# Two feed-forward steps and the end of a recurrent block in another order, and the first weights cast by VectorE

## What is computed

```
def _sq_relu_mlp(x, w1, w2):
    return jnp.square(jax.nn.relu(x @ w1)) @ w2

y = (b_gate * conv3(c_gate * h)) @ w_out                  # layer 1, [b_gate, c_gate, h] = x @ w_in
x = _layer_norm(ALPHA * x + y, ln_mix_g[i], ln_mix_b[i])  # layers 1 and 2
x = _layer_norm(ALPHA * x + _sq_relu_mlp(x, ff_w1[i], ff_w2[i]), ln_ff_g[i], ln_ff_b[i])
x = x + gate[:, None, :] * y                              # layers 3 and 4
k, v = jnp.split(h @ w_kv, 2, axis=-1)                    # h: x normed, scaled and shifted
```

## Time and profile before

| | us |
|---|---|
| median of the timed runs (3) | 780.31 |
| lowest and highest | 780.28, 780.37 |
| the profiled execution, in all | 780.2 |
| its span, from the first to the last instruction | 778.4 |
| TensorE busy in it | 768.9 |
| VectorE busy | 586.1 |
| ScalarE busy | 405.1 |
| GpSimd busy | 34.6 |

### The profile page before, as it was taken

One profiled execution on the slowest core, in us unless ns is written; L12 is line 12 of the kernel. 1 busy time (PEld: TensorE's weight loads), 2 busy tenths in 40 slices (PEclk: granted clock), 3 DMA queues, 4 the chain that ended last, 5 costly groups with the idle time before them and its releaser, 6 DMA issues.

```text
span 778.4 us, 12084 instructions
## 1 busy us (share of the span) xinstructions
PE 768.9 (99%) x4982; PEld 697.1 (90%) x4982; DVE 586.1 (75%) x786; ACT 405.1 (52%) x512; POOL 34.6 (4%) x66
## 2 busy tenths in 40 slices
PE   9999999999999999999999999999999999999996
PEld 9999888988998889888889988998799988999995
DVE  5886898868688697687989776676687877756754
ACT  5455235545445424875355444445649869664632
POOL 0000000000000001000000000000500051000001
PEclk9999999999999999999999999999999999999999
DMA  9877438897867731446488977876235254754102
GB/s 351 319 274 278 184 125 324 348 320 289 313 231 288 290 122 62 163 139 267 165 326 344 347 273 275 308 263 245 103 109 216 109 216 163 270 216 164 55 3 80
DMA packets 26983, 173.94 MB, mean 223 GB/s; under 512 B 3248, under 2 KB 3632, under 8 KB 7856
## 3 DMA queue, kind: packets, MB, share of 16 engines
q1 hardware_dynamic: 26640, 173.14, 60.0%
q10 hardware_dynamic: 288, 0.02, 0.0%
HBM read 172.10 MB, written 1.05 MB: 222 GB/s over the span
## 4 chain that ended last, share of the span: by engine, by line
PE 93%; DVE 3%; ACT 2%; POOL 1%; issue 0%; POOLq 0%; ACTq 0%
PE bank L578 12%; PE bank L580 12%; PE bank L579 12%; PE Y L714 10%; PE Y L716 10%; PE Y L713 10%; PE bank L1067 2%; PE bank L1068 2%; PE bank L1069 2%; PE bank L996 2%; DVE w_low L1610 1%; PE bank L816 1%; PE Y L738 1%; PE bank L610 1%; PE bank L619 1%; PE bank L611 1%
## 5 line engine op out<-in xcount | busy, mean ns | idle before, releaser
L1610 DVE TENSOR_TENSOR w_low<-raw,w_high 128x2048 fp32r<-128x2048 f32 (+3 forms) x125 | 278.5, 2238 | 65.1 <-ACT w_high L1203 62.8
L1203 ACT CAST w_high<-raw 128x2048 fp32r<-128x2048 f32 (+3 forms) x125 | 232.5, 1869 | 92.9 <-DMA raw<-weights 80.0
L578 PE MATMUL bank<-xT_h,w_high 128*128 128x256 f32 x728 | 206.5, 284 | 0.1
L579 PE MATMUL bank<-xT_l,w_high 128*128 128x256 f32 x728 | 205.8, 283 | 0.0
L580 PE MATMUL bank<-xT_h,w_low 128*128 128x256 f32 x728 | 205.8, 283 | 0.0
L578 PEld LDWEIGHTS bank<-xT_h,w_high 128*128 128x128 f32 x728 | 139.4, 192 | 1.6 <-DVE w_low L1610 0.3
L579 PEld LDWEIGHTS bank<-xT_l,w_high 128*128 128x128 f32 x728 | 139.4, 191 | 1.1
L580 PEld LDWEIGHTS bank<-xT_h,w_low 128*128 128x128 f32 x728 | 139.5, 192 | 0.0
L714 PE MATMUL Y<-w_low,hT_h 128*128 128x512 f32 x324 | 128.3, 396 | 0.0
L713 PE MATMUL Y<-w_high,hT_h 128*128 128x512 f32 x324 | 128.0, 395 | 0.0
L716 PE MATMUL Y<-w_high,hT_l 128*128 128x512 f32 x324 | 101.9, 395 | 0.0
(11 more groups left out here) (291 smaller groups left out, 1144.5 us busy)
## 6 DMA issues: line engine op xcount, KB each, us to landing
raw<-weights SPq DMA_DIRECT2D x149, 1024.0 KB, 5.0
rows<-rows_in SPq DMA_DIRECT2D x9, 512.0 KB, 7.7
raw<-weights SPq DMA_DIRECT2D x4, 576.0 KB, 3.5
z<-gates_in SPq DMA_DIRECT2D x4, 512.0 KB, 3.8
raw<-weights SPq DMA_DIRECT2D x2, 896.0 KB, 4.4
raw<-weights SPq DMA_DIRECT2D x3, 512.0 KB, 7.0
x<-x_in SPq DMA_DIRECT2D x2, 512.0 KB, 4.4
kT<-rows_in SPq DMA_DIRECT2D x2, 512.0 KB, 8.3
```

The source lines that it names most:

```text
L578: mm(dst, high, xh[:, kt, :], start=kt == 0, stop=False)
L579: mm(dst, high, xl[:, kt, :], start=False, stop=False)
L1203: nc.scalar.copy(w_high[:, n % RING, start:COLS[n]], raw[:, s % RAW, start:COLS[n]]).then_inc(w_high_ready, 1)
L1610: tt(w_low[:, n % RING, start:COLS[n]], slot[:, start:COLS[n]], f32(w_high[:, n % RING, start:COLS[n]]), ALU.subtract).then_inc(raw_done, 1)
```

## The change

It has three parts.

1. In both feed-forwards, TensorE's order: the first half of group 2's block 0 is done ahead of the transposes of block 1, the second half behind them, and in the same way the first half of group 2's block 1 ahead of `turn_pair` of the first pair.
2. At the end of rg, the splits of the value pieces: VectorE makes the low part of the second piece ahead of the gated residual, the third where the second stood, and the fourth where the third stood. ScalarE casts the third ahead of the squares and the fourth where the third stood.
3. At the beginning, the high part of the first 512 columns is made by VectorE in place of ScalarE (semaphore `first_high`), and the low part of the next 512 columns by GpSimd in place of VectorE (semaphore `second_low`). SyncE waits for `second_low` before it loads into that raw buffer again.

The diff, without the lines that declare the two semaphores:

```diff
             for s, (kind, n) in enumerate(STREAM):
                 if s >= RAW:
                     sp.wait_ge(raw_done, s - RAW + 1)
+                if s == RAW:
+                    sp.wait_ge(second_low, 1)
...
-                    pe.wait_ge(half_high, k0 // 4 + 1)
+                    pe.wait_ge(half_high if k0 else first_high, 1)
...
-                    pe.wait_ge(half_low, k0 // 4 + 1)
+                    pe.wait_ge(second_low if k0 else half_low, 1)
...
                 if n == 1:
-                    pe.wait_ge(half_low, 3)
+                    pe.wait_ge(half_low, 2)
...
                 pair_block(first[0], phase, 0, fresh)
+                up_block(first[2], PI[phase, "up", 2], 0, fresh, range(0, KT // 2))
                 transposes(fresh, x, "x_ready", [1])
-                up_block(first[2], PI[phase, "up", 2], 0, fresh)
+                up_block(first[2], PI[phase, "up", 2], 0, fresh, range(KT // 2, KT))
                 pair_block(first[1], phase, 1, fresh)
+                up_block(first[2], PI[phase, "up", 2], 1, fresh, range(0, KT // 2))
                 turn_pair(phase, 0)
                 in_order(phase, 2)
-                up_block(first[2], PI[phase, "up", 2], 1, fresh).then_inc(product, 1)
+                up_block(first[2], PI[phase, "up", 2], 1, fresh, range(KT // 2, KT)).then_inc(product, 1)
                 turn_pair(phase, 1)
...
+            pool.wait_ge(half_high, 1)
+            nc.gpsimd.tensor_tensor(w_low[:, 0, 512:PIECE // 2], raw[:, 0, 512:PIECE // 2],
+                                    w_high[:, 0, 512:PIECE // 2].bitcast(F32), ALU.subtract).then_inc(second_low, 1)
             pool.wait_ge(ident_in_done, 16)
...
-            part_high(0, 0, 0, 512)
             await_transposed(act, "init", 1, 1)
...
-            split_ahead(("rg", "down", MXG - 1), 2)
+            split_ahead(("rg", "down", MXG - 1), 3)
             rms_squares("rs2", "rg", 0)
...
-            split_ahead(("rg", "down", MXG - 1), 3)
+            split_ahead(("rg", "down", MXG - 1), 4)
             gate_kept(0)
             rms_squares("rs2", "rg", 1)
-            split_ahead(("rg", "down", MXG - 1), 4)
             rms_scale("rs2", 1)
...
-                dve.wait_ge(half_high, part + 1)
+                if part == 0:
+                    dve.wait_ge(first_high, 1)
+                else:
+                    dve.wait_ge(half_high, part)
...
             low_transposed("init", 0)
+            dve.wait_ge(part_in[0], 16)
+            nc.vector.tensor_copy(w_high[:, 0, 0:512], raw[:, 0, 0:512]).then_inc(first_high, 1)
             for q in range(2):
...
-                part_low(q, 0, q * 512, (q + 1) * 512)
+                if q == 0:
+                    part_low(0, 0, 0, 512)
...
-            split_ahead(("rg", "down", 3), 1)
+            split_ahead(("rg", "down", 3), 2)
             gated_residual("rg", 0, 0)
             await_rstd("rs2", 0)
-            split_ahead(("rg", "down", 3), 2)
+            split_ahead(("rg", "down", 3), 3)
```

1 line of the change is left out of this document (added).

## The result

The changed kernel takes 782.01 us in the median, beside 780.32 for the kernel before on the same chip: a ratio of 1.0019, with an interval of 1.0012 to 1.0025, or +1.5 us (+0.9 to +2.0); the two medians by themselves are 1.7 us apart. One of the 18 timed runs took 1526 us, the other 17 took 781.0 to 782.6; it doesn't move the median. The forecast was 781.5, in a range of 780.5 to 782.7. By the bound of 0.2% this is right at the edge between no change and slower.

A forecast was written before the change was run, and what follows sets the result against it. TensorE, busy 768.9 of 778.4 us, was taken as the bound. Terms 0.66 + 0.34 − 0.13 + 0.34 = +1.21 us; 780.2 + 1.2 + 0.1 = 781.5 us, range 780.5 to 782.7.

The forecast's parts named there:

- ff1, +0.66: Second feed-forward: removing the wait for x gives 0.84 us, later VectorE work up to turned_low(1) takes back 1.50.
- ff0, +0.34: First feed-forward: no wait to remove; later turn_pair(0) and ScalarE's cast delay turned_low, so down(0, 1) starts +0.34 us.
- The end of rg, −0.33 + 0.20: Value pieces: wait for v2's w_low goes, −0.33 us; GpSimd's columns wait out VectorE's w_low, root +0.20 us.
- The beginning, +0.34: GpSimd's subtraction holds VectorE's big low part until 11.07, so the second tile starts at 12.34, not 12.00: +0.34 us.
- (b): Beginning: GpSimd and VectorE don't hold each other; second tile at 11.91, −0.09 us, in all 781.1; chance 0.16.
- (a): Beginning: GpSimd gets in ahead of VectorE's first low part; second tile 12.98, +0.98 us, in all 782.2; chance 0.26.
- Rival (d): Beginning: GpSimd shut out, losing to VectorE piece by piece; second tile at 15.4, +3.4 us, in all 784.6; chance 0.08.
- Rival (c): Feed-forwards: VectorE takes the later transposes without being late; sum −1.26 us, in all 779.0; chance 0.08.
- the wait before turn_pair(1): Sign in ff1: TensorE waits about 0.65 us for VectorE before turn_pair(1), in place of the wait for x.
- those before down(0, 1): Sign in both feed-forwards: TensorE waits for VectorE before down(0, 1).
- ff1's down(0, 1) 0.3 us farther from ff0's: Sign across the feed-forwards: the distance between the two down(0, 1) starts grows by 0.3 us.
- the second tile at 12.3: Sign at the beginning: the second tile at 12.3 us, with a GpSimd subtraction of 1.8 us including its wait.

The follow-up runs named there:

- ff_only: Part 1 alone (TensorE's order in both feed-forwards) on the kernel before: 781.61 us, ratio 1.0016.
- half_a: Kernel before with only part 1's half block ahead of the transposes of x: one run, ff0 +0.40, ff1 +0.74 us.
- half_b: Kernel before with only part 1's half block ahead of turn_pair of the first pair: one run, ff0 +0.52, ff1 +0.46 us.
- rg_columns_early: Part 2 on the kernel before, plus GpSimd spreading the second gate's columns into buf_a after the recurrent layer's first quarter: 779.82 us, ratio 0.9991.
- ff_late_mod: Part 1 on the kernel before, plus VectorE's modulation piece ahead of group 2's squares moved behind turned_low(1): 780.68 us, ratio 1.0001.
- start_only: Part 3 alone (the beginning) on the kernel before: 780.56 us, ratio 1.0001.
- rg_and_between: Kernel before with parts 1 and 2, one VectorE weight piece behind turned_low(0), the rest behind turned_low(1), GpSimd's columns early: 779.78 us, ratio 0.9994.
- hold: Kernel before plus four extra GpSimd 128x512 two-input subtractions beside VectorE's work at the beginning: one run, second tile at 14.08 us.
- all_repaired: All three parts on the kernel before, with ff_squares_first's VectorE order and rg_columns_early's edit: 780.91 us, ratio 1.0008.
- ff_squares_first: Part 1 on the kernel before, plus VectorE's weight and modulation pieces between the squares put off behind turned_low(1): 781.02 us, ratio 1.0005.
- rg_only: Part 2 alone (the value pieces at the end of rg) on the kernel before: 780.29 us, ratio 0.9998.

## Why the prediction was right, and where not

**ff1, +0.66: right, measured +0.75.** Each step is in the rows: the wait for x gone, xT_l at 379.34, 2.69 us behind the last of the pair's products (376.65), by the forecast 378.39 − 375.69 = 2.70. Down to turned_low(1) nothing gave. From the pair's end to down(0, 1) it is 393.92 − 376.65 = 17.27 us, and was 392.29 − 375.69 = 16.60: +0.67. Of the rest, 0.1 is the restart: down(0, 1)'s first products are 0.57 us apart behind the wait (393.40 and 393.97 in ff_only) and 0.48 without one. half_a shows that the late xT_l alone does it.

**ff0, +0.34: right, measured +0.50.** From the pair's end (107.55, the 106.64 of its low products plus 0.91) to down(0, 1) it is 123.67 − 107.55 = 16.12 us, beside 122.82 − 107.06 = 15.76: +0.36, and 0.1 for the same restart. half_b shows that the path named, by `turn_pair` and the cast, costs this by itself. What the forecast didn't see is that half_a alone costs +0.40 too, though its own terms say so: xT_l comes 1.44 us later and finds 0.21 us of idle time, which leaves 1.23, beside 1.24 by way of the cast. The delayed xT_l brings turned_low(0) to the same time (118.94 and 118.96), so undoing either half alone would not have saved ff0.

**The end of rg, −0.33 + 0.20: the mechanism right, the second term mis-sized.** The wait for v2 went, for −0.41 (the 0.33, and a restart that went with it). GpSimd did wait out the added w_low. But the forecast let it in between VectorE's two pieces, and had the root 0.2 us late. One column lasted 4.52 us, through both of them; the root came 643.22 − 632.15 = 11.07 us behind the first column, and was 640.89 − 630.42 = 10.47 behind it: 0.6 us late, not 0.2. In the stage table the transposes of z are 0.44 late. The sum is +0.03, where the forecast had −0.13. rg_columns_early takes the collision away and leaves −0.43, which settles it.

**The beginning, +0.34: the number came near (+0.48) by luck, its reason did not take place.** The step that failed is the time at which the operations meet. The forecast took ScalarE's times from the earlier trace rows; in the changed kernel everything behind the second x block is some 0.6 us later, because its load is. GpSimd starts at 9.97, beside an xT_l with an input in PSUM. By the time it is through (11.30), VectorE's big low part has just started, at 11.20, held by ScalarE's cast and that by its load. None of VectorE's operations there is longer than in the earlier trace rows by more than 0.01 us, so of the rivals (b) fits the edit best. (a) did not occur: VectorE's first low part starts at 9.46, 0.5 us ahead of GpSimd.

What the 0.48 us measure is two late loads. TensorE's first tile, late by x, runs up to the second one without idle time. And the load of the rest of piece 0 would have put the second tile there by itself: ScalarE's cast waits for it until 10.12, and the same delay stands in ff_late_mod and in rg_columns_early, which have the old beginning. Of ff_late_mod:

```profile
10.08 1.05 ACT L1205 CAST w_high<-raw 128x1024 fp32r<-128x1024 f32 x1 [0.31 <-DMA raw<-weights]
...
12.44 0.39 PE L578 MATMUL bank<-xT_h,w_high 128*128 128x256 f32 x1 [0.43 <-DVE w_low L1612]
```

From the start of this cast to the second tile it is 2.36 or 2.37 us in ten of the fourteen profiles, the changed kernel, start_only and eight with the old beginning. It is 2.42 in the kernel before, 2.54 in rg_and_between, 4.37 in `hold`, and 2.53 in all_repaired, the one place where part 3's own hold shows: 0.16 us. Measured from the first tile instead, the second comes 2.97 us later in the changed kernel and 3.16 in the one before. That says little, since with the old beginning it is 3.09 to 3.57, by when the loads came.

That the two engines hold each other was right, as `hold` shows, and the Trainium skill, page "SBUF — State Buffer", section "SBUF: two separate sides", says it: of a GpSimd operation and a VectorE operation with two inputs in SBUF, whichever starts first has the shared ports for its whole instruction. The runs agree: 1.0 us for each VectorE operation beside one of GpSimd's, and none for the one with a PSUM input.

What stays open is why the loads come when they do. For the weights the spread is there with the old beginning too. TensorE transposes the second x block at 7.54, 7.60 and 7.16 in the three profiles with part 3, and at 6.19 to 7.02 in the six others whose rows show it apart. Part 3 changes nothing that comes before these loads in any queue. With three profiles the late x can be chance; or it can be something that the trace doesn't show. The timed runs of start_only put it and everything else of part 3 within 0.7 us of nothing.

**Rival (d)**, GpSimd shut out for long, is refuted for two-input operations: in `hold` they go by turns. **Rival (c)** fell by ff0 and ff1, as above.

**What would show it.** Of the signs, the wait before turn_pair(1) came as 0.51 us of idle time, or 0.66 from start to start, and those before down(0, 1) came as well. One sign was miscounted: the forecast has ff1's down(0, 1) 0.3 us farther from ff0's, but ff0's shift moves both, so by its own terms it is 0.66. Measured it is (393.92 − 123.67) − (392.29 − 122.82) = 0.78. The sign that the second tile at 12.3 speaks for the hold was no test, since the loads alone put it at 12.44 and 12.47 in kernels with the old beginning.

**The range and the chances.** The parts sum to +1.76 us in the profile and the timed runs show +1.5. Against the profile the forecast's +1.21 was low by 0.25 in the feed-forwards (0.2 of it two restarts), by 0.16 at the end of rg, and by 0.14 at the beginning. Without the beginning, the parts sum to 1.76 − 0.48 = 1.28 us. The forecast had 0.66 + 0.34 − 0.13 = 0.87 for the same three places, so by the mechanism it was 0.4 us low, and the term of the beginning covered most of that.

## What to carry to other kernels

A wait that is taken away by doing later work first is only moved if the engine behind it has no idle time: read that engine's rows from the moved step to its next consumer, in every place that runs the same code, and add up the idle time in the brackets before counting the gain. When work on a feeding engine is put off, ask when its buffer comes free and how long the load behind takes, not only when its result is needed. And when VectorE's program is filled up beside GpSimd's, look for what GpSimd does in those microseconds; moving its columns out of the way turned part 2 from nothing into −0.43 us in the profile. Last, before a change is charged with a difference at the start of a kernel, see how far the first loads move it in profiles without the change: here by 0.6 us.

## What the runs showed of the hardware

- A wait of TensorE costs more than the idle time in its row. One of 0.51 us (ff_late_mod beside ff_squares_first) cost 0.92: 0.66 until the next start and 0.26 in the instructions behind it. The Trainium skill, page "TensorE: Matmul & The Clock Gate", section "Step-by-step: what each phase is for", has a reason: back to back, the drain of one matmul lies under the fill of the next. That a wait costs something beyond itself agrees with it; no run here separates the parts of the 0.92.
- GpSimd's one-input operation (a column of 128x128, 0.60 us alone) beside VectorE's w_low took up to 4.52 us in the changed kernel, through two VectorE operations in a row, and VectorE's first one was 2.38 us long beside 2.28 for the second. In `hold` two-input operations of GpSimd took turns with VectorE's instead, and each of VectorE's was 1.0 us longer.
- A GpSimd subtraction of 128x512 takes 1.33 us (forecast 1.1) and a VectorE cast of 128x512 takes 0.43 us (forecast 0.44), both in the changed kernel.
- The first loads do not land at the same time in every run. With the same beginning, ScalarE's cast of the rest of piece 0 started at 9.46 without a wait in rg_and_between, and at 9.61, 9.62, 10.08 and 10.10, waiting for its load, in half_b, rg_only, ff_late_mod and rg_columns_early. In the ten profiles with the old beginning and without `hold`'s extra work, TensorE's second tile came 2.36 to 2.54 us behind it.
